# The sample group's expert rows: U rows one by one into block 2's V pass, V rows directly behind it

## The reference

```python
    idx = jnp.take_along_axis(cand_i, best_pos, axis=-1)
    g = jax.nn.softmax(best_s, axis=-1)
    u = peer_u[idx]
    a = jax.nn.gelu(jnp.einsum('nd,nhkd->nhk', xb, u).astype(jnp.float32), approximate=False)
    v = peer_v[idx]
    return jnp.einsum('nhk,nhkd->nd', g * a, v.astype(jnp.float32)).astype(xb.dtype)
```

## Time and profile before

| | |
|---|---|
| median of 3 runs | 2263.88 us (2257.58 to 2264.44) |
| the profiled execution, its own time | 2264.58 us |
| its span | 2262.8 us |
| mean granted TensorE clock | 0.818 |
| busy: PE / DVE / POOL / ACT | 66% / 61% / 47% / 9% |
| DMA moved | 726.19 MB, mean 321 GB/s |
| gathers of `peer_u` and `peer_v` | 520 + 520 |

### The profile page before, as it was taken

The page is one execution under the profiler, slowest core; times in us unless marked ns, Lnnn a source line. Parts: engine busy times, 40 slices in busy tenths (PEclk is TensorE's granted clock), DMA queues, the critical chain, the costliest instruction groups (busy, mean ns, idle before and its releaser), DMA issues.

```text
span 2262.8 us, 17470 instructions
## 1 busy us (share of the span) xinstructions
PE 1504.3 (66%) x6048; PEld 661.3 (29%) x6048; DVE 1382.4 (61%) x3124; ACT 202.9 (9%) x444; POOL 1068.0 (47%) x1126
## 2 busy tenths in 40 slices
PE   6999678988747654979895003995004999200998
PEld 3444342454533332223453001221001222000222
DVE  2878952253588767610489999973999402999000
ACT  3113300002100220000201000000000000100000
POOL 0311113100105555433333777777776774777773
PEclk9999789969879776899998556998556997655999
DMA  7776438645538897996684999999999998999998
GB/s 262 269 290 259 172 116 317 254 157 189 197 137 323 331 406 284 395 349 260 235 323 158 392 409 409 409 409 410 409 410 409 409 409 340 362 411 410 409 409 329
DMA packets 208424, 726.19 MB, mean 321 GB/s; under 512 B 20192, under 2 KB 25056, under 8 KB 197968
## 3 DMA queue, kind: packets, MB, share of 16 engines
q0 software_dynamic: 160368, 616.91, 69.9%
q1 hardware_dynamic: 39776, 99.22, 12.0%
q10 hardware_dynamic: 8192, 8.95, 1.1%
HBM read 714.96 MB, written 10.04 MB: 320 GB/s over the span
## 4 chain that ended last, share of the span: by engine, by line
PE 49%; DVE 18%; DMA 16%; POOL 10%; issue 5%; ACT 2%; SPq 0%; ACTq 0%; DVEq 0%; POOLq 0%
PE ps L1806 19%; PE ps L1589 15%; DMA arena<-in_peer_u,arena 10%; POOL arena L599 10%; DVE arena L1257 9%; DMA arena<-in_peer_v,arena 4%; PE ps L1966 3%; DVE arena L943 2%; PE ps L1696 1%; DMA arena<-in_cache_diff_v,arena 1%; PE ps L1983 1%; PE ps L1550 1%; PE ps L1872 1%; PE ps L1991 1%; ACT ps L641 1%
## 5 line engine op out<-in xcount | busy, mean ns | idle before, releaser
L599 POOL DMA_INDIRECT arena<-in_peer_u,arena x520 | 487.9, 938 | 478.6 <-DVE arena L1257 200.5
L1257 DVE CUSTOM_DVE_ANT_0 arena<-arena,ps 128x1024 f32<-128x1024 f32 x512 | 608.4, 1219 | 41.8 <-DMA arena<-in_peer_u,arena 29.2
L599 POOL DMA_INDIRECT arena<-in_peer_v,arena x520 | 491.2, 945 | 289.0 <-PE ps L1806 170.1
L1806 PE MATMUL ps<-arena 128*32 128x512 f32 x2048 | 580.6, 618 | 10.0 <-DMA arena<-in_peer_v,arena 8.4
L1589 PE MATMUL ps<-arena 128*128 128x512 f32 x960 | 434.7, 609 | 7.9 <-ACT arena L651 5.0
L1797 PE MATMUL ps<-arena 128*128 128x128 f32 x4 | 1.9, 476 | 481.3 <-DVE arena L943 481.3
L1806 PEld LDWEIGHTS ps<-arena 128*32 128x32 f32 x2048 | 163.6, 112 | 421.2 <-issue 305.3
L1589 PEld LDWEIGHTS ps<-arena 128*128 128x128 f32 x960 | 182.9, 194 | 238.0 <-issue 230.0
L943 DVE TENSOR_TENSOR arena<-arena,ps 128x512 f32<-128x512 f32 (+6 forms) x59 | 48.9, 831 | 283.7 <-PE ps L1806 163.4
L943 DVE TENSOR_TENSOR arena<-arena 128x256 f32<-128x256 f32 (+7 forms) x339 | 196.9, 608 | 23.2 <-DMA arena<-in_state_ret 5.7
L1797 PEld LDWEIGHTS ps<-arena 128*128 128x128 f32 x4 | 0.7, 183 | 484.3 <-DVE arena L943 484.3
(11 more groups left out here) (229 smaller groups left out, 1281.6 us busy)
## 6 DMA issues: line engine op xcount, KB each, us to landing
arena<-in_w_pq SPq DMA_DIRECT2D x8, 2048.0 KB, 15.1
arena<-in_w_in SPq DMA_DIRECT2D x7, 2048.0 KB, 10.9
arena<-in_peer_u,arena POOLq DMA_INDIRECT x520, 11.0
arena<-in_peer_v,arena POOLq DMA_INDIRECT x520, 16.4
arena<-in_w_out SPq DMA_DIRECT2D x4, 2048.0 KB, 8.4
arena<-in_w_mq SPq DMA_DIRECT2D x4, 2048.0 KB, 13.0
arena<-in_w_mo SPq DMA_DIRECT2D x4, 2048.0 KB, 14.3
arena<-in_cache_mem_k SPq DMA_DIRECT2D x8, 1024.0 KB, 8.0
```

Of the source, the lines that this page charges most:

```text
L599: return pool.indirect_dma_start(slot, None, table[0], bass.IndirectOffsetOnAxis(idx.bitcast(U32), 0))
L1257: dve.tensor_tensor_reduce(row, row, x_copy(b), 1.0, 0.0, ALU.mult, ALU.add, DOTS[:, k:k + 1]).then_inc(s["u_used"], 1)
L1806: last = pe.matmul(PS[32 * j:32 * j + 32, 6 + half, :], window(n, i, j), row[:, 512 * half:512 * half + 512], start=(n == 0 and i == 0), s ...
```

## The change

The table `ORDER` of whole blocks becomes `RUNS`, a table of runs of rows. Behind the first 40 V rows of block 2, each of the sample's 8 U rows goes before an eight of block 2's V rows; then follow block 2's last 24 V rows, the sample's V rows, and block 3 as before. TensorE's list follows: broadcast k stands before eight 5 + k of the V pass, block 3's numbers are turned behind eight 13, and the sample's V rows come right behind the pass. On VectorE `turned_numbers(3)` and `add_expert_rows(2)` go behind the sample's weights.

```diff
-ORDER = [("u", 0), ("v", 0), ("u", 1), ("v", 1), ("u", 2), ("v", 2), ("u", SMP), ("v", SMP), ("u", 3), ("v", 3)]
+SMP_STEP = 5
+RUNS = [("u", 0, 0, P), ("v", 0, 0, P), ("u", 1, 0, P), ("v", 1, 0, P), ("u", 2, 0, P),
+        ("v", 2, 0, SMP_STEP * CHUNK),
+        *(run for k in range(DB) for run in (("u", SMP, k, k + 1), ("v", 2, (SMP_STEP + k) * CHUNK, (SMP_STEP + k + 1) * CHUNK))),
+        ("v", 2, (SMP_STEP + DB) * CHUNK, P), ("v", SMP, 0, DB), ("u", 3, 0, P), ("v", 3, 0, P)]
...
 def used_through(kind, b):
-    return sum(DB if c == SMP else P for k, c in ORDER[0:ORDER.index((kind, b)) + 1] if k == kind)
+    end = max(i for i, run in enumerate(RUNS) if run[0:2] == (kind, b)) + 1
+    return sum(k1 - k0 for k, _, k0, k1 in RUNS[0:end] if k == kind)
...
@@ block.vector @@
             gate_args(3)
-            turned_numbers(3)
-            add_expert_rows(2)
             for b in range(DB):
                 row = row_landed(dve, "u", SMP, b)
                 dve.wait_ge(s["xb_ready"], b + 1)
...
             tt(SWM, mask8, sgl.unsqueeze(2).broadcast_to([P, DB, DB]), ALU.mult).then_inc(s["weight_ready"], 1)
+            turned_numbers(3)
+            add_expert_rows(2)
             dot_products(3, 0, NSEL // 4)
...
@@ block.tensor @@
+            def sample_x(k):
+
+                pe.wait_ge(s["u_used"], used_through("u", 2) + max(k - 1, 0))
+                for i in range(2):
+                    last = pe.matmul(PS[:, 2 * (k % 2) + i, :], sel[0:DB, k, :], QR[0:DB, SMP, 512 * i:512 * i + 512],
+                                     start=True, stop=True)
+                last.then_inc(s["xb_ready"], 1)
+
             for b in range(1, NBLK):
-                numbers_turned(b)
-                if b == 3:
-                    for k in range(DB):
-                        pe.wait_ge(s["u_used"], used_through("u", 2) + max(k - 1, 0))
-                        for i in range(2):
-                            last = pe.matmul(PS[:, 2 * (k % 2) + i, :], sel[0:DB, k, :], QR[0:DB, SMP, 512 * i:512 * i + 512],
-                                             start=True, stop=True)
-                        last.then_inc(s["xb_ready"], 1)
+                if b < 3:
+                    numbers_turned(b)
+                weights_turned(b)
...
+                pe.wait_ge(s["y_ready"], PICKS.index(b))
+                for n in range(NSEL // CHUNK):
+                    if b == 2 and SMP_STEP <= n < SMP_STEP + DB:
+                        sample_x(n - SMP_STEP)
+                    expert_rows(b, n)
+                    if b == 2 and n == SMP_STEP + DB:
+                        numbers_turned(3)
+                if b == 2:
                     pe.wait_ge(s["u_used"], used_through("u", SMP))
                     pe.wait_ge(s["weight_ready"], PICKS.index(SMP) + 1)
                     for k in range(DB):
...
```

More of the change, by code:

```diff
@@ L148, in plan_gathers @@
     i = 0
-    for kind, b in ORDER:
+    for kind, b, k0, k1 in RUNS:
         if (kind, b) == ("u", 1):
             i = 0
-        for k in range(DB if b == SMP else P):
+        for k in range(k0, k1):
             slot = i % (9 if b == 0 else 17)
@@ L1975, in _ @@
                     numbers_turned(0)
-            for b in range(1, NBLK):
-                numbers_turned(b)
-                if b == 3:
-                    for k in range(DB):
-                        pe.wait_ge(s["u_used"], used_through("u", 2) + max(k - 1, 0))
-                        for i in range(2):
-                            last = pe.matmul(PS[:, 2 * (k % 2) + i, :], sel[0:DB, k, :], QR[0:DB, SMP, 512 * i:512 * i + 512],
-                                             start=True, stop=True)
-                        last.then_inc(s["xb_ready"], 1)
+            def sample_x(k):
[4 more added lines that the diff above has]
+                last.then_inc(s["xb_ready"], 1)
+            for b in range(1, NBLK):
+                if b < 3:
+                    numbers_turned(b)
+                weights_turned(b)
+                if b == 2:
+                    pe.wait_ge(s["gates_done"], PICKS.index(SMP) + 1)
+                    pe.transpose(PS[:, 5, 0:DB], sidx_row[0:DB, :], ident[0:DB, 0:DB])
+                    pe.transpose(PS[:, 5, P:P + DB], GATE[0:DB, SMP, :], ident[0:DB, 0:DB]).then_inc(s["idx_turned"], 1)
+                pe.wait_ge(s["y_ready"], PICKS.index(b))
[5 more added lines that the diff above has]
+                        numbers_turned(3)
+                if b == 2:
                     pe.wait_ge(s["u_used"], used_through("u", SMP))
@@ L1993, in _ @@
                         last.then_inc(s["v_used"], 1)
[L1994 to L2001, removed]
 _INS = ["x_prompt", "x_sample", "mem_prompt", "cache_diff_k", "cache_diff_v", "page_table", "state_ret", "cache_mem_k",
```

## The result

The changed kernel takes 2256.3 us (median of 7 runs, 2253.0 to 2260.0) against 2263.9 for the kernel before (7 runs, 2257.0 to 2268.6): ratio 0.997, interval 0.9956 to 0.9984. It is faster, by 7.6 us (0.3%) and not by the 16.2 that were forecast; 2256.3 lies inside the range, near its upper end, where the rival "VectorE bounds block 3's U pass" gave 2256.1. The profiled execution took 2254.8 us, its span 2253.0.

A forecast was written before the change was run, and what follows sets the result against it. The prediction took the stream of expert rows at 410 GB/s as the bound. Profiled 2264.58 us less 16.2, all other terms 0, gave 2248.4; against the median 2263.88 this was 2247.7 us, range 2241.4 to 2257.1.

The forecast's parts named there:

- VectorE bounds block 3's U pass: Rival: VectorE limits block 3's U pass, so only its 7.8 us earlier start is gained; 2256.1 us, chance 0.04.
- The gain: Stretch 1905 to 1945 us: its 9.76 MB would stream at 410 instead of 244 GB/s, saving 16.2 us.
- The queue's cover: Block 2's V pass: 12.5 us of queue hide V slots freed up to 3.4 us late; cost 0, uncovered 3.4 us.
- U slots: Block 2's V pass: the sample's U row slots free in time, as VectorE is idle there; cost 0.
- Broadcasts: TensorE, block 2's V pass: 3.4 us a step; with eight V rows 7.4 of the 11.5 us available.
- Sample weights: Around the end of block 2's V pass: weights ready some 14 us before TensorE wants them; cost 0.
- sample V pass: Directly behind block 2's V pass: 8 rows at 1.72 us, 13.8 in all; block 3's U row 16 has 8.6 us to spare.
- late release: Rival: the sample's V rows, 3.41 us each at 1.2 GHz, free their slots 4.9 us late; 2252.6 us, chance 0.08.
- First dot product of block 3: Start of block 3's U pass on VectorE: U row 0 was to land at 1910.8 us.
- the last dot product: End of block 3's U pass on VectorE: forecast near 2073.7 us, 16.2 us earlier than 2089.9.
- the lost overlap: Rival, block 2's V pass: V rows stop overlapping after full-width broadcasts; 16 us slower, about 2280 us, chance 0.05.

## Why the prediction was half right

**What failed is the step "The gain".** It took the 40 us at 244 GB/s, a mean over 16 DMA engines, for what rows had to wait: 16.2 us. A row waits for its slowest engine, and that one stood 8.8 us behind when the dent began and used 7.3 of it. Its own loss was 8.9; measured are 8.8 in the trace and 7.6 between medians. The rest of the term doesn't vanish, it moves to the end. By the 5 us rows the mean stream is through at about 2230 + 5 x 203 / 410 = 2232.5, before at 2250 + 6 x 35 / 410 = 2250.5: 18 us earlier, 17 beside the V pass's own start. But behind it 11.5 us of one engine's lag are still to come where there were 2.7, and 17 - 8.8 is 8.2, close to the 8.8 measured.

**The queue's cover** was read wrongly from the same cause. Of the 17.7 us from issue to landing I took 12.5 as queue on every engine. By the events of these rows the first engine was done 9.0 us after the issue and the 15th 12.3; with a dry queue (the row issued at 1926.55) it was 4.0 and 4.9. So 15 of the engines had 5 to 7 us of queue, not 12.5. Nothing came of it here, since POOL never waited longer than 0.8 us for a used slot from 1775 to 1945.

**Right, by the trace:**
- U slots: free in time; POOL waited 3.5 us for them in all, 0.7 at most.
- Broadcasts: 11.5 us apart, as forecast, and no cost even when doubled. The price of a step was too high in the forecast: 1.72 us of matmuls and 1.68 of drains, where the step took 1.98 us in TensorE's timeline and 1.91 in the chain. The 0.84 us of the earlier trace rows are idle time of the weight loads, and hardly of the matmuls. The Trainium skill, TensorEngine Tiling (Array Packing), Tiling Modes, has the engine drained at each change of mode; with 16 changes no run here shows any cost in the kernel's time, and on TensorE itself they took about 8 x (1.98 - 1.72) = 2.1 us, not 13.4.
- Sample weights and sample V pass: 32 matmuls in 13.9 us against 13.8, clock 1.00; no late release behind it.
- First dot product of block 3 at 1910.05 against 1910.8; VectorE never the bound (half its work changed nothing).
- Not right: the last dot product, 2080.3 against 2073.7. This is the 7 us of the failed step.

**The rivals.** Late release, VectorE and the lost overlap did not happen; VectorE's 2256.1 hits the median by chance. No rival had the mechanism, and the earlier trace rows could not have shown it by themselves: 17.7 us to land in one pass and 5.2 after a dent is a short queue as well as a lag that is gone, and block 3's V pass before the change has 17.7 us again with a lag of 2.7. It takes the 16 events of each row.

**Semaphores.** The Trainium skill, DMA: Bandwidth & Descriptors, "Why a DMA increments its semaphore by 16 and not by 1", says that the engines finish independently and only the full 16 mean that all has landed. The trace agrees, and its events give the size, up to 12.4 us between the first and the last in the median of 50 us (15.1 for a single row).

**Open.** Why 8 KB hold one engine for 0.97 us: at a sixteenth of 410 GB/s they would take 0.32, and the packet's own record says 0.34. Which physical engine it is, the trace doesn't say; that it carries VectorE's instructions follows from the 1024 and the 384 added instructions. Whether a kernel with fewer VectorE instructions is faster in the median was not settled, and fewer instructions in the selection were not tried.

## What to carry to other kernels

Before a dent in the mean throughput is counted as loss, compare the first and the last of the 16 landing events of the same gathers ahead of it and behind it: if the distance falls, here from 8.8 to 1.5 us, a lagging engine has caught up, and only the rest of the dent can be had back. Issue to landing is not enough, since the queue is in it. At the end of a stream, read the throughput in 5 us windows; a sixteenth of the full rate for 10 us is one engine that is late; that its lag can be had back as time is shown in a trace, not in a median. Where a long DMA stream bounds, the number of instructions of an idle engine is a cost: here 0.97 us for 128 of VectorE's, and nothing for 384 of ScalarE's.

## What the runs showed that was not expected

- A packet of 8192 bytes of VectorE's instructions puts one of 16 DMA engines 0.97 us behind, and this adds up to 12.4 us (median of 50 us); other packets of the same queue, those of 384 ScalarE instructions among them, and q8's of 16384 bytes did not.
- 1024 one-element copies on an engine that was otherwise idle cost 7.1 us.
- TensorE's clock stayed at 1.00 with eight single broadcasts 11.5 us apart, but in the bunch of the same eight it was 1.00 until 1787 us and 0.50, the level of 1.2 GHz, from 1789 on, and they took 23.1 us where 8 x 1.98 are 15.8. With each broadcast doubled, spread out as they are, the mean from 1750 to 1850 was 0.90.
